# A hybrid decoder layer on one core: the second index block of the first projection moved ahead of both memory blocks, and loads of the decode index heads moved from the second stage into the first

## The reference, cut to what matters

```python
u = rmsnorm(x, g_pre);  P = u @ w_in         # gates i and f, index q (8 heads x 64), index k (64), index w (8), ...
ig = P.ml_i + b; lf = log_sigmoid(P.ml_f + b)               # gates of the mLSTM, running maxima over tokens
qi, ki = rope(P.idx_q), rope(P.idx_k)                       # rotary on the index heads and the index key
ki_all = concat(cache_kidx[page_table], ki)                 # decode: 8192 cached index keys per sequence, in pages
score = sum_h w_h * relu(qi_h . ki_all);  idx = top_k(score)
mem_k, mem_v = rmsnorm(mem) @ w_mem_k, rmsnorm(mem) @ w_mem_v   # 256 memory tokens, outputs of the layer too
```

## Time and profile before

| what | us |
|---|---|
| median of three runs | 2778.8 (2774.35 to 2779.37) |
| the profiled execution | 2776.92 |
| its span in the trace | 2775.0 |
| last matmul of the first stage ends | 235.5 |
| first transpose of the second stage | 242.05 |
| first transpose of page part 1 | 262.29 |
| PE busy | 2706.0, 98% of the span |

### The profile page before, as it was taken

One profiled execution on the slowest core, in us unless ns is written; L12 is line 12 of the kernel. 1 busy time (PEld: TensorE's weight loads), 2 busy tenths in 40 slices (PEclk: granted clock), 3 DMA queues, 4 the chain that ended last, 5 costly groups with the idle time before them and its releaser, 6 DMA issues.

```text
span 2775.0 us, 35939 instructions
## 1 busy us (share of the span) xinstructions
PE 2706.0 (98%) x13915; PEld 1927.0 (69%) x13915; DVE 1247.3 (45%) x2149; ACT 581.4 (21%) x1369; POOL 408.3 (15%) x826
## 2 busy tenths in 40 slices
PE   7998999999999999999999999999989999899998
PEld 6674468856854488888888888888755555455553
DVE  3242589867854754132232234453232232345553
ACT  3122458860000000000011100100232222222211
POOL 0000014320000000000000022330113300333341
PEclk9999999999999999999999999999999999999999
DMA  6457312212221312322332344563574411975652
GB/s 225 111 151 249 116 33 76 68 49 71 85 80 60 117 45 63 85 64 70 121 111 77 93 141 145 160 186 105 176 248 146 145 51 51 297 230 171 208 168 84
DMA packets 272709, 341.99 MB, mean 123 GB/s; under 512 B 40892, under 2 KB 225460, under 8 KB 267260
## 3 DMA queue, kind: packets, MB, share of 16 engines
q1 hardware_dynamic: 238940, 262.19, 30.2%
q0 software_dynamic: 16528, 67.92, 8.0%
q10 hardware_dynamic: 17072, 9.58, 1.2%
HBM read 262.16 MB, written 80.01 MB: 123 GB/s over the span
## 4 chain that ended last, share of the span: by engine, by line
PE 86%; SPq 2%; DMA 2%; DVE 1%; issue 1%; ACT 0%; POOL 0%; DVEq 0%; ACTq 0%
PE sbank L1491 44%; PE sbank L1488 10%; PE kept_bank L3299 8%; PE kept_bank L2251 7%; PE sbank L1371 2%; PE at_bank_dots L2233 1%; PE kept_bank L2279 1%; PE mo_bank_dots_num L3264 1%; PE mo_bank_kv L3275 1%; PE sbank L1334 1%; PE sbank L1256 1%; PE mo_bank_kv L3322 1%; PE at_bank_turn L2219 1%; DMA attention_then_units<-gate_rows 1%; PE at_bank_dec L2309 1%
## 5 line engine op out<-in xcount | busy, mean ns | idle before, releaser
L1491 PE MATMUL sbank<-w,xT 128*128 128x256 f32 x3200 | 699.8, 380 | 0.0
L1491 PEld LDWEIGHTS sbank<-w,xT 128*128 128x128 f32 x3200 | 607.3, 190 | 83.6 <-issue 3.3
L1491 PE MATMUL sbank<-w,area 128*128 128x256 f32 x1664 | 361.4, 380 | 0.0
L1971 DVE TENSOR_TENSOR pout_b<-pout_b,sbank 128x256 f32<-128x256 f32 x320 | 134.4, 421 | 498.8 <-PE sbank L1491 410.2
L1491 PEld LDWEIGHTS sbank<-w,area 128*128 128x128 f32 x1664 | 316.6, 190 | 42.0
L1934 DVE TENSOR_TENSOR w<-w 128x2048 f32<-128x2048 f32 x63 | 142.9, 2289 | 318.9 <-PE sbank L1491 255.7
L1586 ACT ACTIVATE pout_b<-sbank 128x256 f32<-128x256 f32 x120 | 45.1, 382 | 890.6 <-PE sbank L1491 658.4
L1491 PE MATMUL sbank<-w 128*128 128x256 f32 x832 | 181.9, 380 | 2.6 <-issue 2.6
L1491 PEld LDWEIGHTS sbank<-w 128*128 128x128 f32 x832 | 158.3, 190 | 23.8 <-issue 2.8
L1488 PE MATMUL sbank<-xT,w 128*128 128x512 f32 x384 | 166.6, 593 | 0.0
L1488 PEld LDWEIGHTS sbank<-xT,w 128*128 128x128 f32 x384 | 72.9, 190 | 90.0 <-issue 89.9
(11 more groups left out here) (483 smaller groups left out, 3445.1 us busy)
## 6 DMA issues: line engine op xcount, KB each, us to landing
w<-in_w_in SPq DMA_DIRECT2D x64, 1024.0 KB, 5.3
proj<-pout_b SPq DMA_DIRECT2D x208, 128.0 KB, 1.7
area<-in_x_prompt SPq DMA_DIRECT2D x16, 1024.0 KB, 7.4
attention_then_units<-proj SPq DMA_DIRECT2D x128, 128.0 KB, 3.1
area<-roped_q_of_decode POOLq DMA_DIRECT2D x32, 256.0 KB, 4.0
w<-in_w_out SPq DMA_DIRECT2D x4, 2048.0 KB, 15.3
y_of_groups_b_c<-out_parts SPq DMA_DIRECT2D x32, 256.0 KB, 2.3
mo_dec_states<-in_state_mlstm_C SPq DMA_DIRECT2D x32, 256.0 KB, 6.3
```

The costliest lines, as they stand in the source:

```text
L1491: last = nc.tensor.matmul(bank[t][:, 0:256], x(c, t * P, (t + 1) * P), at[name][:, c, :], start=first_ and c == 0, stop=c == 7, skip_group ...
L1971: nc.vector.tensor_tensor(out[:, t, :], x[:, t, :], product_at(n, t), ALU.add).then_inc(sums_read, 1)
```

## The change

The order of blocks becomes block 0, second index block (tiles 9 to 17), MEM_K (18, 19), MEM_V (20, 21). `gates.load` is issued before the weights of the next block; the weights of MEM_V are loaded after `load_r` of the last tile. The three `gates.scalar` stand before the copies of tiles 12, 12 and 14. `turned_at` has new places. The decode heads, the key and `pick` are loaded at the end of the first stage, into memory (`k.sck`, `k.rbias`) that outlives it; the first gather moves behind all kidx stores; in the second stage POOL and DVE no longer wait for these loads. Tile 9 no longer waits for the copies of the memory rows; tile 11 does.

```diff
-    BLOCKS = [[(C_IQ, 288), (C_I, 8)], [(MEM_K, HW)], [(C_IQ + 288, 296)], [(MEM_V, HW)]]
+    BLOCKS = [[(C_IQ, 288), (C_I, 8)], [(C_IQ + 288, 296)], [(MEM_K, HW)], [(MEM_V, HW)]]
-    GATES, INDEX, LAST = 1, 2, 3
+    INDEX, KEYS, LAST = 1, 2, 3
...
-            i, v = fp.FIRST[fp.INDEX], fp.FIRST[fp.LAST]
-            return {i + 5: {4: 0, 14: 1}, i + 6: {8: 2, 15: 3}, i + 7: {8: 4}, i + 8: {0: 5}, v: {2: 6, 7: 7, 12: 8}}.get(m, {})
+            i, mk = fp.FIRST[fp.INDEX], fp.FIRST[fp.KEYS]
+            return {i + 6: {8: 0, 15: 1}, i + 7: {6: 2, 13: 3}, mk: {0: 4, 4: 5, 8: 6, 13: 7}, mk + 1: {5: 8}}.get(m, {})
...
-            sp.wait_ge(done, fp.FIRST[1])
+            stores_landed(fp.FIRST[fp.INDEX])
             sp.wait_ge(normed, ROWS)
-            load_w(2, 0)
-            load_w(2, 1)
-            stores_landed(fp.FIRST[fp.GATES])
             sp.wait_ge(turned, ROWS)
             gates.load(sp)
-            for m in range(fp.FIRST[1], fp.FIRST[2]):
+            sp.wait_ge(done, fp.FIRST[fp.INDEX])
+            load_w(fp.KEYS, 0)
+            load_w(fp.KEYS, 1)
+            for m in range(fp.FIRST[fp.INDEX], fp.FIRST[fp.KEYS]):
                 store(m)
+                if m == fp.FIRST[fp.INDEX] + 4:
+                    gates.store(sp)
+                if m > fp.FIRST[fp.INDEX]:
+                    load_r(m - fp.FIRST[fp.INDEX] - 1)
+            load_r(QT)
             load_w(fp.LAST, 0)
             load_w(fp.LAST, 1)
...
+            store(fp.FIRST[fp.KEYS])
             sp.wait_ge(iws_out, 16 * DEC_B)
...
+            sp.dma_start(k.pick[:, :, :], ins["pick"].rearrange("p (s c) -> p s c", s=2)).then_inc(heads_in, 16)
+            sp.wait_ge(r_stored, 32 * N_TILES)
+            for s2 in range(2):
+                half = slice(64 * s2, 64 * s2 + 64)
+                for par in range(2):
+                    sp.dma_start(k.qi4[half, par, :, :], k.headT[64 * par:64 * par + 64, T_IQ:T_IK, SEQ:TOK]
+                                 ).then_inc(heads_in, 16)
+            sp.dma_start(k.ktn[0:64, :], k.headT[0:IDX_D, T_IK, SEQ:TOK]).then_inc(heads_in, 16)
+            for m in range(fp.FIRST[fp.KEYS] + 1, fp.ALL):
+                store(m)
...
-                if n == 7:
-                    pool.wait_ge(done, fp.FIRST[fp.LAST])
-                    nc.gpsimd.indirect_dma_start(
+            pool.wait_ge(done, fp.FIRST[fp.LAST])
+            nc.gpsimd.indirect_dma_start(
...
-                if m == fp.FIRST[fp.GATES] + 2:
+                if m == fp.FIRST[fp.INDEX] + 3:
                     gates.scalar(act, 0)
-                if m == fp.FIRST[fp.GATES] + 3:
                     gates.scalar(act, 1)
-                if m == fp.FIRST[fp.GATES] + 5:
+                if m == fp.FIRST[fp.INDEX] + 5:
                     gates.scalar(act, 2)
...
-                if m == N_TILES + 1:
+                if m == N_TILES + 2:
                     pe.wait_ge(kept_a, 2 * ROWS)
...
-                    pe.wait_ge(kept_a, 2 * ROWS - 2)
-                    pe.wait_ge(kept_v, 2 * ROWS - 2)
...
-            pool.wait_ge(const, 16 * 5)
             for p in range(1, 4):
...
-            dve.wait_ge(const, 16 * 5)
             for q in range(2):
                 nc.vector.tensor_copy(qz[...], qi4[...])
             keep_keys(1)
-            dve.wait_ge(pick_in, 16)
```

More of the change, by code:

```diff
@@ L283 @@
     MEM_K, MEM_V = -1, -2
-    BLOCKS = [[(C_IQ, 288), (C_I, 8)], [(MEM_K, HW)], [(C_IQ + 288, 296)], [(MEM_V, HW)]]
+    BLOCKS = [[(C_IQ, 288), (C_I, 8)], [(C_IQ + 288, 296)], [(MEM_K, HW)], [(MEM_V, HW)]]
     N_B = len(BLOCKS)
-    GATES, INDEX, LAST = 1, 2, 3
-    PIECES = {0: (4, (0, 14016)), 1: (2, (2368, 6464)), 2: (2, (11648, 14016)), 3: (2, (0, 4096))}
+    INDEX, KEYS, LAST = 1, 2, 3
+    PIECES = {0: (4, (0, 14016)), 1: (2, (2368, 4736)), 2: (2, (8192, 12288)), 3: (2, (0, 4096))}
     def __init__(self):
@@ L358, in project_index @@
     ix_ord = S("ix_rotary_order")
-    iws_out = S("iws_stored")
+    iws_out, heads_in = S("iws_stored"), S("decode_heads_loaded")
+    k.qi4 = k.sck.rearrange("p u (j n) -> p u j n", n=NS)
+    k.ktn, k.pick = k.rbias[:, 0:NS], k.rbias[:, NS:NS + 16].rearrange("p (s c) -> p s c", s=2)
     (k.pti_in,), (k.wcol_in,), k.pages = k.queue_sems("pti_loaded", 1), k.queue_sems("wcol_loaded", 1), k.queue_sems("pages_loaded", 2)
@@ L533, in _ @@
                              k.proj[SEQ + DEC_T * s:SEQ + DEC_T * (s + 1), C_IW:C_MQ]).then_inc(iws_out, 16)
-            for m in range(fp.FIRST[3], fp.ALL):
-                store(m)
+            store(fp.FIRST[fp.KEYS])
             sp.wait_ge(iws_out, 16 * DEC_B)
@@ L541, in _ @@
                                  ).then_inc(k.wcol_in, 16)
+            sp.dma_start(k.pick[:, :, :], ins["pick"].rearrange("p (s c) -> p s c", s=2)).then_inc(heads_in, 16)
[8 more added lines that the diff above has]
+                store(m)
+            sp.wait_ge(heads_in, 16 * 6)
             for j in range(P_BANKS):
@@ L562, in _ @@
                                     ).then_inc(kidx_stored[n % 2], 16)
-                if n == 7:
-                    pool.wait_ge(done, fp.FIRST[fp.LAST])
-                    nc.gpsimd.indirect_dma_start(
-                        out=flat[:, 8192:16384], out_offset=None, in_=ins["cache_kidx"][:, :],
-                        in_offset=bass.IndirectOffsetOnAxis(ap=k.pti[:, 0:1], axis=0)).then_inc(k.pages[0], 16)
+            pool.wait_ge(done, fp.FIRST[fp.LAST])
+            nc.gpsimd.indirect_dma_start(
+                out=flat[:, 8192:16384], out_offset=None, in_=ins["cache_kidx"][:, :],
+                in_offset=bass.IndirectOffsetOnAxis(ap=k.pti[:, 0:1], axis=0)).then_inc(k.pages[0], 16)
             for u in range(2):
@@ L800, in select @@
     fq = Quads()
-    const, small, pick_in = S("select_consts"), S("select_small"), S("pick_loaded")
+    small = S("select_small")
     pages = k.pages
@@ L876, in select @@
         cidx = k.sb("cidx", [P, TOPK], U32, at=st)
-        qi4 = vals[:, :].rearrange("p (u j n) -> p u j n", u=2, n=NS)
-        ktn = k.sb("ktn", [P, NS], at=st)
+        qi4, ktn, pick = k.qi4, k.ktn, k.pick
         rn = k.sb("rn", [P, 16], at=st)
         iw = k.sb("iw", [P, 6, IDX_H], at=st)
-        pick = k.sb("pick_sb", [P, 2, 8], at=st)
         nbias = k.sb("nbias", [P, DEC_T], at=st)
@@ L976, in _ @@
         def _(sp):
[L977 to L983, removed]
             for s2 in range(2):
```

## The result

The changed kernel takes 2796.2 us (median of seven, 2786.6 to 2801.8), the one before 2777.5 (seven runs, 2773.7 to 2789.2). The ratio is 1.0064 with a 95% interval of 1.0051 to 1.0076: **slower by 0.6%, by more than was forecast and outside the range**. The profiled execution took 2794.59 us, its span is 2792.7; against the 2775.0 before that is +17.7, where the sum said +5.8.

A forecast was written before the change was run, and what follows sets the result against it. It took PE, busy 98% of the span, as the bound, so only PE's gaps could change. First stage +11.7, passage -2.0 and -3.9, sum +5.8 us: 2782.7 against the profiled execution, given as 2784.6, range 2777 to 2792.

The forecast's parts named there:

- the sum: Whole kernel: +11.7 to the first stage's end, -2.0 and -3.9 in the passage, together +5.8 us.
- Gap at 99.9, removed: First stage, after block 0: PE's 2.62 us idle goes, and 1.9 us of clock loss with it.
- Their chain, the wait at tile 15: Transposes of rotated tile 0: PE waits 12.2 us, from 153.8 to 166.0, for the gate loads and rotation 0.
- Second wait: Before rotated tile 3 (tile 16): PE waits 2.9 us more for its load, and the clock falls again, 1.9.
- rival (b): At rotated tile 3: no second wait and no clock fall, total +1.0, 2779.8 us; chance 0.15.
- rival (a): At the second wait: the clock doesn't fall, total +3.9, 2782.7 us; chance 0.20.
- To the end, "they are covered": Rest of the first stage: rotations 4 to 8 cause no wait; matmuls end at 247.2, +11.7 against before.
- Rival (c): Late first stage: stores of turned heads slowed beside MEM_V's weights, 7 us more, +12.8, 2791.6 us; chance 0.12.
- Passage: First stage's end to part 1: next stage at 4.5 (-2.0), first dot product 5.4 in, part 1 16.3 in (-3.9).
- Rival (d): Second stage: page part 1 is late, total +11.1, 2789.9 us; chance 0.05.

The follow-up runs named there:

- e4: The kernel before, with POOL gathering page part 1 without waiting for the loads of the heads; 2787.3 us, ratio 1.0031.
- e3: The changed kernel with one of the two transposing gate loads replaced by a load of contiguous rows (forget gate left out); 2787.0 us, one run.
- g9: The changed kernel with wcol by 32 direct loads instead of the eight copies, and MEM_V's weights behind the store of tile 18; 2790.5 us, one run.
- f5: The changed kernel with wcol read by 32 small loads straight from the projection, without the eight index-weight copies; 2792.0 us, one run.
- e1: The changed kernel with the eight index-weight copies and the wcol loads moved behind the loads of the decode heads; 2793.6 us, ratio 1.0048.
- e2: The changed kernel with the loads of MEM_V's weights moved behind the store of tile 18; 2799.5 us, one run.
- g8: The changed kernel with direct wcol loads, MEM_V's weights earlier, and rotated tiles' transposes later, spread by their stores' time; 2770.2 us, 0.9959 of before.

## Why the prediction was right and wrong

Against the profiled execution the sum was +5.8 and the trace has +17.7. By its own steps:

- **Gap at 99.9, removed**: right. Tile 9 follows at 99.69 with no idle time. The 1.9 us of clock in it hold for the profiled execution before and not for every one: in e4, which has the same gap of 2.62, the clock stayed at 1.00 and the half tile behind it took 7.11 instead of 8.80.
- **Their chain, the wait at tile 15**: right, 12.40 for 12.2. `gates.load` is issued at 105.79 (106 forecast), rotation 0 starts at 163.40 (163.5); the two loads took 13.96 and 14.85 us. The case that the fit of the Trainium skill (DMA: Bandwidth & Descriptors, Anatomy of one DMA) would have made, an estimated 4 us for both and a faster kernel, is refuted again by these rows; the page gives that fit for transfers issued by GpSimd, and these are SP's. e3 shows that the loads are what made the wait.
- **Second wait**: right in size, 3.08 for 2.9, and rival (b) is out. The clock fell, so rival (a) is out too. The size was taken whole from a row of before, and what is in that row is more than SP's list: behind the last of the gates' stores (`out_sample_m`, 32 single values transposed into memory) there is a silence of 1 to 2 us in both kernels, and the packets of the load of rotated tile 3, begun just before it, last up to 5. Windows, kernel before:

```profile
182.00:184.00 2.00, 2.00 (x10) 1.53 (x9) 0.00 (x0) 0.70 (x3) 0.00 (x0) 1.00 0.00 1
```

- **To the end, "they are covered"**: this is **the step that failed**. It counted rotations and loads of rotated tiles 4 to 8, and left out the stores of turned heads, each of which holds ACT's next copy. Waits of 0.41, 2.73 and 7.19, 10.3 together, and one more fall of the clock (0.50 in the windows from 218 on, some 1.9 us by the price used before) make the 12.1 us between 247.2 and 259.3.
- **Rival (c)** had the place and the mechanism, with 0.12 and a price of 7. It was too cheap twice: it saw one store slowed and not two, and only the weights. Of the 12.1, g9 against f5 gives 3.4 to the weights, and f5 against the changed kernel 6.8, of which 4 or more are the copies of single values; e1 (6.0 for moving them) and e2 point the same way. The diff moves these eight DMAs with the rest of SP's list from behind most stores to the middle of them. The prediction had no term for them.
- **Passage**: right, the stage starts at +3.8 for +4.5, the first dot product comes 4.9 us into it for 5.4, part 1 16.9 for 16.3; together -6.15 for -5.9. Rival (d) is out, and e4 shows that the early gather alone is a loss. The first gather was hidden, as said.
- **Sum**: 12.1 more in the first stage, 0.25 less in the passage: +17.7.

The Trainium skill (DMA: Bandwidth & Descriptors, Issuing engines are not separate DMA queues) says that transfers of different issuers share the same 16 engines and interleave. The traces agree that SP's traffic reaches ACT's store. By this rule I had weighed (c) down, since I took a store of 256 KB that takes its turns to need a few us, which the page doesn't say; measured, it held ACT for 8.07 and 9.39 beside the weights (e1, f5), and for 14.05 with the copies. The landing of the heads' stores in the changed kernel (and of the five loads that read them), from 150 to 240, has a median of 2.4:

```profile
DMA to landing us min/median/max: 1.8/2.4/13.5
```

The 13.5 at its end, the store of tile 6, is the worst of what the step left out.

## What to carry to other kernels

A step that waits for its own store has the queues' load in its price. When such a chain is moved, list what will be in flight beside each of its transfers at the new place: big loads that were once elsewhere, and above all writes of single values to memory, however few bytes they carry. Places written out by hand pay twice for being early, once for the wait and once for the clock behind it; here moving them later, the weights earlier, and dropping eight tiny copies turned +18.6 us into -11.3.

## What was not expected of the hardware

- After eight copies of 32 single values each, from memory to memory in a transposed order, nothing or next to nothing moves on any queue for 6 to 10 us, beginning within 5 us of the last one's issue: 213 to 219 in the changed kernel, 228 to 238 in e1, 205 to 211 in e2, 200 to 208 in e3, 217 to 224 in the kernel before. It followed the copies to each place, and without them stores out at those places were not held so (g8, g9: 2.6 to 3.0 us). That they are the cause is shown; what in the chip stands still isn't. An empty window alone proves nothing: f5 has one from 218 to 226, when only the 32 small loads were out.
- The same happens in small behind the gates' last store, 32 single values from the core's own memory to a transposed place in memory: packets of 2304 bytes, some 0.1 us elsewhere, last 2 to 5 us. They begin 1.1 to 1.2 us after that store's issue ends at each of three places: at 181.2 before (store issued at 179.8), 174.1 after (172.6), 160.0 in e3 (158.6). No run takes this store away, so it is a reading of three traces and not shown.
- Loads of the same index weights straight into the core's own memory, 16 values to a DMA, do not do this (g8: holds of 2.7 to 3.0 us among them).
- 8 KB behind a 4 MB gather took 11.6 us (e4), 2.1 before.
- The clock is not told by a wait's length alone. Behind waits of 2.48 (e1), 2.53 (f5) and 2.62 (before) the granted clock fell to 0.50; the 0.83 of the earlier trace rows, which the prediction took for the level, is the mean of the microsecond in which it fell. Behind the same 2.62 in e4, 2.73 (after), 2.78 and 2.89 (g9) it stayed at 1.00. Every wait of the first stage from 3.08 us on lost it.
